# Right-sum transfers into gate and up, border loads and turns in another order, and first sums of an FFN made in the output projection

## The reference

```python
def causal_dwconv(x, w, b):            # width 3 along the tokens, per channel
    ...
def conv_ffn(h, w_gate, w_up, conv_w, conv_b, w_down):
    g = causal_dwconv(h @ w_gate, conv_w, conv_b)
    return (jax.nn.gelu(g) * (h @ w_up)) @ w_down

for i in range(DEPTH):                 # DEPTH = 2, D_FF = 2816
    h = rmsnorm(x, norm_mix[i])
    x = x + mixer(h, ...) @ w_out[i]
    h = rmsnorm(x, norm_ffn[i])
    x = x + conv_ffn(h, w_gate[i], w_up[i], conv_w[i], conv_b[i], w_down[i])
    gate = jax.nn.sigmoid(rmsnorm(x, norm_ple[i]) @ w_ple_gate[i])
    x = x + gate * (p[i] @ w_ple_proj[i])
```

## Time and profile before

| what | value |
|---|---|
| runs | 3158.32, 3159.48, 3169.77 us; median 3159.48 |
| profiled execution, own time | 3161.22 us |
| its span | 3159.2 us |
| PE busy | 3014.0 us, 95% |
| DVE, ACT, POOL busy | 2271.2, 1444.3, 1403.9 us |
| mean granted TensorE clock | 0.979 |

### The profile page before, as it was taken

How to read it: one execution, slowest core, us unless ns; L and a number is a source line. 1 busy time by engine, 2 the same in 40 slices (tenths; PEclk the granted TensorE clock), 3 DMA queues, 4 the chain that set the end, 5 groups by cost and what they waited for, 6 DMA issues and landing times. The chain is left out here.

```text
span 3159.2 us, 44227 instructions
## 1 busy us (share of the span) xinstructions
PE 3014.0 (95%) x14830; PEld 2520.0 (80%) x14830; DVE 2271.2 (72%) x3459; ACT 1444.3 (46%) x3125; POOL 1403.9 (44%) x905
## 2 busy tenths in 40 slices
PE   7999889999999999999899999999998999999989
PEld 6777777989877888878788788899886888878877
DVE  6599957879458887779943332799648888779952
ACT  4384435878343343334432211688633333434431
...
GB/s 179 122 61 164 140 181 122 60 54 78 116 54 80 80 84 82 127 246 193 99 61 37 195 178 170 81 66 80 54 88 54 96 82 80 81 240 197 157 48 53
DMA packets 288086, 349.07 MB, mean 110 GB/s; under 512 B 88316, under 2 KB 181292, under 8 KB 287916
## 3 DMA queue, kind: packets, MB, share of 16 engines
...
## 5 line engine op out<-in xcount | busy, mean ns | idle before, releaser
L2162 DVE TENSOR_SCALAR_CACHE_REDUCE k_x<-k_x,l0in_cand,l0in_want 128x384 bf16<-128x384 f32 (+1 forms) x186 | 175.0, 1004 | 1.2 <-DVE l0in_before L2157 0.2
L78 PE MATMUL l1in_acc<-k_w_lo,k_hi 128*128 128x512 f32 x384 | 151.7, 395 | 5.2 <-POOL k_w_lo L681 2.7
L2648 POOL TENSOR_TENSOR l1ff_w_lo<-l1ff_raw_g,l1ff_w_hi 128x512 fp32r<-128x512 f32 x64 | 93.5, 1466 | 138.6 <-ACT l1ff_w_hi L2511 138.5
L2648 POOL TENSOR_TENSOR l0ff_w_lo<-l0ff_raw_g,l0ff_w_hi 128x512 fp32r<-128x512 f32 x64 | 91.9, 1438 | 140.8 <-ACT l0ff_w_hi L2511 140.7
L2540 ACT ACTIVATE k_x<-k_x 128x512 f32<-128x512 f32 x88 | 55.7, 633 | 212.3 <-DVE k_x L2742 212.3
L79 PE MATMUL l1in_acc<-k_w_hi,k_lo 128*128 128x512 f32 x384 | 150.8, 393 | 0.0
L80 PE MATMUL l1in_acc<-k_w_hi,k_hi 128*128 128x512 f32 x384 | 150.6, 392 | 0.0
L725 DVE TENSOR_TENSOR l1in_sq<-l1in_out 128x512 f32<-128x512 f32 x32 | 40.4, 1264 | 114.7 <-ACT l1in_out L658 114.0
L1619 DVE TENSOR_TENSOR l1dil_pt_lo<-l1dil_ring,l1dil_pt_hi 128x512 fp32r<-128x512 f32 x192 | 101.9, 553 | 4.6 <-ACT l1dil_pt_hi L1555 2.3
L1635 DVE CUSTOM_DVE_ANT_0 l1dil_s<-l1dil_s,l1mix_sliding 128x128 f32<-128x128 f32 (+7 forms) x128 | 97.3, 761 | 9.0 <-PE l1dil_s L1719 4.7
L1555 ACT ACTIVATE l1dil_pt_hi<-l1dil_ring 128x512 fp32r<-128x512 f32 x192 | 92.5, 492 | 22.6 <-PE l1dil_ring L1702 21.4
...
## 6 DMA issues: line engine op xcount, KB each, us to landing
l_right_sums<-in_w_down POOLq DMA_DIRECT2D x24, 1408.0 KB, 14.0
...
k_raw<-in_w_in_odd SPq DMA_DIRECT2D x24, 512.0 KB, 4.9
l0ff_raw_g<-in_w_gate SPq DMA_DIRECT2D x11, 1024.0 KB, 5.2
l0ff_raw_u<-in_w_up SPq DMA_DIRECT2D x11, 1024.0 KB, 5.6
...
l1ff_raw_g<-in_w_gate SPq DMA_DIRECT2D x11, 1024.0 KB, 5.2
```

The costliest lines, as they stand in the source:

```text
L78: pe.matmul(out, a_hi, b_lo, start=start, stop=False)
L2162: tick(dve.tensor_scalar(hits[:, cols], score[:, cols], cand[:, i:i + 1].bitcast(F32), want[:, i:i + 1], ALU.is_ge, ALU.add, accum_out=exc ...
L2648: pool.tensor_tensor(buf.ring_lo[q % R][:], operand(q), buf.ring_hi[q % R][:].bitcast(F32), ALU.subtract).then_inc(w_lo_done[0], 1)
```

## The change

1. The twelve right-sum transfers of each layer leave the input projection. They are issued in gate and up, one each after steps n = 6 and n = 13 of a group, copies in groups 0 to 2, adds in groups 3 to 5.
2. The output stage's POOL program makes the first group's sums for factors 7 and 5 and, for token tiles 4 and 5, the differences that factors 6 and 7 need. The sums are formed in other places: factor 7 in piece (0,0), 5 in piece (1,0), 6 in tmp.
3. The FFN's start has another order: on POOL `root(LAST)` first; on DVE the differences of tile 6 alone, then scale(LAST), and the rest later; on PE turn(LAST) in the middle of step 2 instead of between steps 1 and 2.
4. SP's order at the border of up and down: a11 parts 8 to 10 and a12 part 8 are loaded before the last stores, the parts of a22 and the x tiles one by one between the down loads, and load_down(7) comes right after the last store.
5. The embedding's turns come after parts 7 and 9 of the last down product instead of 6 and 8, and the first waits for all adds but two.

```diff
# projection_stage and project_select_stage, POOL
-                    if s == 1 and t < right_sums.count:
-                        right_sums.copy(pool, t)
-                    if s == 3 and t < right_sums.count:
-                        right_sums.add(pool, t)
...
# SplitFeed
+    def differences(self, engine, t):
+
+        n = t - max(self.first, self.EARLY)
+        front, rear, early = self.raw[self.part(t, 0)], self.raw[self.part(t, 1)], self.raw[self.part(t - self.EARLY, 0)]
+        engine.wait_ge(self.summed, n + 1)
+        engine.wait_ge(self.rested, 2 * max(self.EARLY - self.first, 0) + n + 1)
+        engine.tensor_tensor(front, rear, front, ALU.subtract).then_inc(self.differed, 1)
+        engine.wait_ge(self.differed, 2 * n + 1)
+        engine.tensor_tensor(rear, rear, early, ALU.subtract).then_inc(self.differed, 1)
...
# output_stage, POOL
+            for m in range(2):
+                pool.wait_ge(n_lo_ready, m + 1)
+                pool.tensor_tensor(nxt.piece(m, 0, 0), nxt.piece(m, 0, 0), nxt.piece(m, 1, 0), ALU.subtract).then_inc(n_w_sum, 1)
+                pool.wait_ge(n_w_sum, 2 * m + 1)
+                pool.tensor_tensor(nxt.piece(m, 1, 0), nxt.piece(m, 1, 0), nxt.piece(m, 1, 1), ALU.add).then_inc(n_w_sum, 1)
             for t in range(nxt.ROOTS):
                 nfeed.root(pool, t)
+            for t in range(NT // 2, NT // 2 + 2):
+                nfeed.differences(pool, t)
...
# ffn_stage, SP
+                if q == Q - 1:
+                    sp.wait_ge(filled, Q - 2)
+                    load_part(a11, (0, 0), range(8, 11), a11_in)
+                    load_part(a12, (0, 1), range(8, 9), a12_in[1])
...
-            load_part(a22, (1, 1), range(4, 8), a22_in)
...
             for z in range(DEEP + 3, Z):
                 r, k = divmod(z, KB2)
                 load_down(z)
...
+                if (r, k) == (0, 7):
+                    sp.wait_ge(stored[0], 16 * 2 * NG)
+                    load_part(a12, (0, 1), range(9, 11), a12_in[2])
+                    sp.wait_ge(stored[1], 16 * 2 * NG)
+                    sp.wait_ge(filled, Q)
+                if 8 <= z <= 11 or z in (14, 16, 18, 20):
+                    t = z - 8 if z <= 11 else z // 2 - 3
+                    sp.dma_start(x[:, t, :], buf.kept[t * P:(t + 1) * P, :]).then_inc(x_in[t // 4], 16)
+                if 9 <= z <= 11 or z in (13, 15, 17, 19):
+                    i = z - 5 if z <= 11 else z // 2 + 1
+                    load_part(a22, (1, 1), range(i, i + 1), a22_in)
...
# ffn_stage, POOL
             feed.prepare(pool)
-            add_weights(0, 5, 0)
             feed.root(pool, LAST)
-            add_weights(0, 5, 1)
-            add_weights(0, 7, 0)
+            add_weights(0, 6, 0)
             low(4)
-            add_weights(0, 6, 0)
-            add_weights(0, 7, 1)
+            add_weights(0, 6, 1)
...
+                if n in (6, 13) and grp < 6:
+                    i = 2 * (grp % 3) + (n == 13)
+                    right_sums.copy(pool, i) if grp < 3 else right_sums.add(pool, i)
...
# ffn_stage, PE
-            feed.turn(pe, LAST)
-            step(2)
+            step(2, True)
...
-                if r == len(DOWN) - 1 and k in (6, 8):
-                    if k == 6:
-                        pe.wait_ge(added, ADDED[r])
-                    nfeed.turn(pe, (k - 6) // 2)
+                if r == len(DOWN) - 1 and k in (7, 9):
+                    pe.wait_ge(added, ADDED[r] - 2 if k == 7 else ADDED[r])
+                    nfeed.turn(pe, (k - 7) // 2)
```

More of the change, by code:

```diff
@@ L697, in _ @@
                     low(CH * s + c)
-                    if s in (1, 2) and c < right_sums.count // 2:
-                        right_sums.copy(pool, (s - 1) * (right_sums.count // 2) + c)
-                    if s in (3, 4) and c < right_sums.count // 2:
-                        right_sums.add(pool, (s - 3) * (right_sums.count // 2) + c)
                 if s <= QK:
@@ L1930, in _, with project_select_stage @@
             first.begin(pe, hi, lo)
-def project_select_stage(nc, name, right_sums, hi, lo, strips, proj, vsplit, vstored, room, stats, score, mask, tail, square, decay, first, next_head=None):
+def project_select_stage(nc, name, hi, lo, strips, proj, vsplit, vstored, room, stats, score, mask, tail, square, decay, first, next_head=None):
     S = len(strips)
@@ L2545, in difference, with second_high @@
                     act.wait_ge(t1_lo, 1)
-                    act.wait_ge(t_lo_done, 2)
+                    act.wait_ge(t_lo_done, 3)
                 act.activation(t_hi[f][:], t_raw[f], ACT.Copy).then_inc(t_hi_done, 1)
+            def second_high(n):
+                act.wait_ge(t_sum, 2 + 2 * n)
+                act.activation(t_hi[6][:, :, cols[n]], t_raw[6][:, :, cols[n]], ACT.Copy).then_inc(t_hi_done, 1)
             def split_left(z):
@@ L2589, in _ @@
             feed.square(act, LAST)
+            split(3)
+            second_high(0)
             copy_sum(0, 0)
             feed.round(act, LAST)
-            copy_sum(0, 1)
             act.wait_ge(feed.summed, 1)
             act.activation(hi[:, front, 6 * P:], xt[:, front, 2 * P:4 * P], ACT.Copy).then_inc(t1_hi, 1)
-            for q in range(3, L + 1):
-                split(q)
+            split(4)
+            copy_sum(0, 1)
+            second_high(1)
+            split(5)
             for q in range(1, Q + 3):
@@ L2610, in _ @@
                     base(4 * grp + (n == 12))
[L2611 to L2612 removed]
+                if q in (3, 6):
+                    difference(*{3: (7, 4), 6: (4, 5)}[q])
                 if q + L < Q:
@@ L2824, in down_slot, with sums_of, second_low @@
                     nfeed.rest(dve, (k - 8) // 2)
-            cols = slice(0, 3 * P), slice(3 * P, 4 * P)
-            def difference_sums(n):
+            def sums_of(t):
+                at = slice((t - NT // 2) * P, (t - NT // 2 + 1) * P)
                 b11, b12, b22 = xt[:, front, early], xt[:, front, late], xt[:, rear, late]
-                dve.tensor_tensor(b12[:, :, cols[n]], b22[:, :, cols[n]], b12[:, :, cols[n]], ALU.subtract).then_inc(t_sum, 1)
-                dve.tensor_tensor(b22[:, :, cols[n]], b22[:, :, cols[n]], b11[:, :, cols[n]], ALU.subtract).then_inc(t_sum, 1)
-            difference_sums(0)
-            feed.scale(dve, LAST)
+                n = 2 * (t - LAST + 1)
+                dve.tensor_tensor(b12[:, :, at], b22[:, :, at], b12[:, :, at], ALU.subtract).then_inc(t_sum, 1)
+                dve.wait_ge(t_sum, n + 1)
+                dve.tensor_tensor(b22[:, :, at], b22[:, :, at], b11[:, :, at], ALU.subtract).then_inc(t_sum, 1)
+            def second_low(n):
+                dve.wait_ge(t_hi_done, n + 1)
+                dve.tensor_tensor(t_lo[6][:, :, cols[n]], t_raw[6][:, :, cols[n]], t_hi[6][:, :, cols[n]].bitcast(F32),
+                                  ALU.subtract).then_inc(t_lo_done, 1)
+            sums_of(LAST - 1)
+            feed.scale(dve, LAST)
+            low(3)
+            second_low(0)
+            feed.rest(dve, LAST)
+            dve.wait_ge(t1_hi, 1)
+            dve.tensor_tensor(lo[:, front, 6 * P:], xt[:, front, 2 * P:4 * P], hi[:, front, 6 * P:].bitcast(F32), ALU.subtract).then_inc(t1_lo, 1)
+            dve.wait_ge(feed.rested, 1)
+            dve.wait_ge(feed.summed, 1)
+            sums_of(LAST)
+            low(5)
+            second_low(1)
             dve.wait_ge(kept_stored[0], 16 * 6)
@@ L2838, in _ @@
                 dve.memset(g[i][:, 0:2], 0.0)
-            feed.rest(dve, LAST)
-            dve.wait_ge(feed.rested, 1)
-            dve.wait_ge(feed.summed, 1)
-            difference_sums(1)
-            dve.wait_ge(t1_hi, 1)
-            dve.tensor_tensor(lo[:, front, 6 * P:], xt[:, front, 2 * P:4 * P], hi[:, front, 6 * P:].bitcast(F32), ALU.subtract).then_inc(t1_lo, 1)
-            low(3)
-            low(5)
             dve.wait_ge(cw_t, 1)
@@ L2894, in _, with step @@
         def _(pe):
-            def step(q):
+            def step(q, turn=False):
                 grp, f, m = op(q)
@@ L2920, in step @@
                 for k in range(4):
+                    if turn and k == 2:
+                        feed.turn(pe, LAST)
                     mm = mm3(pe, out(grp, f, m), buf.ring_hi[q % R][:, k, :], buf.ring_lo[q % R][:, k, :], b_hi[:, k, :], b_lo[:, k, :],
@@ L3011, in trunk @@
                                   second_at=MERGED_AT + 8 * KB)
-                    projection_stage(nc, L + "in", right_sums[layer], x, heads, ident, proj, vsplit, vstored, stats, dil)
+                    projection_stage(nc, L + "in", x, heads, ident, proj, vsplit, vstored, stats, dil)
                 recycle(nc)
```

80 lines of the change are left out of this document (28 added, 52 removed).

## The result

The changed kernel takes 3135.6 us (median of 5 runs, 3133.9 to 3138.9) against 3158.3 for the kernel before (5 runs): ratio 0.9931, interval 0.9918 to 0.9944. It is faster by 22.7 us. I had forecast 3071, a gain of 88.9 on the 3159.5 of the first three runs, in a range of 3058 to 3106. Where the other 65 us went is the subject of what follows.

A forecast was written before the change was run, and what follows sets the result against it. PE, busy 95% of the span, was taken as the bound, so only its waits counted. Gains 29.5 + 3.8 + 2 x (11.6 + 7.8 + 8.4) = 88.9 off 3159.5 gave 3071 us, range 3058 to 3106.

The forecast's parts named there:

- Right sums in gate and up: In gate and up, 24 right-sum transfers issued one at a time, about 19 us apart, would cost 0.
- The sign that I had named for it: Would show the forecast wrong: a new PE wait for w_lo behind DMA at the heads of groups 1 to 6.
- My upper bound of 14.1: In gate and up, a 5.2 us weight load stretched by 13.3/4.9 beside a transfer would take 14.1, 8.9 more.
- The slack: Gate and up: the second group's load is there about 7.4 us early, so 1.5 of 8.9 would show.
- The right sums cost in gate and up what they cost in the projection: Rival for gate and up: 24 transfers at 1.5 to 2.5 cost 36 to 60, 3107 to 3131 us; chance 0.08.
- Layer 0's projection: Without transfers, PE's three waits at strip heads (22.7) and 7.5 after them go, less about 0.6: gain 29.5 us.
- slow part: What a PE wait costs after its end: 2.5 us for over 4, 1 to 1.6 for 2.7, none under 2.
- the search's cover: In layer 0's projection, DVE's top-k search would still end before ACT, by 1.8 us.
- Layer 1's projection: One PE wait of 2.7 for k_w_lo, with 1.1 lost after it, goes: gain 3.8 us.
- The FFN's start: Step 1 to 12 falls from 48.4 to 34.7 us, less 1.8 at the output stage's end: gain 11.6 per layer.
- The border: From up to down, PE's 5.52 us wait goes as load_down(7) is issued earlier: gain 7.8 per layer.
- The end of down: PE's 8.53 us wait before the next stage's first turn shrinks to 2.2: gain 8.4 per layer.

The follow-up runs named there:

- the quiet places: Changed kernel with copies moved behind steps n = 0 and 1 of groups 1 to 3, adds behind n = 0 of groups 4 to 9: 3078.3 us, ratio 0.9745.

## Why the prediction was wrong

**The step that failed** is "Right sums in gate and up", priced at 0: "One transfer at a time is nearer to layer 1's projection than to layer 0's, so I take 0." It measured 26.8 and 25.9 us in groups 1 to 10 of the two layers, and with the transfers at the quiet places the kernel is 57 us faster. The sign that I had named for it came, a new wait of PE for w_lo, at the heads of groups 2 to 6. Without this cost the time comes near what I had forecast, 3078.3 against 3071. Part of that is luck, since misses cancel: by the profiles of that run and of before, layer 0's projection gave 34.1 where I had 29.5, and the two FFN stages 23.9 and 21.3 where I had 27.8 each.

Three things in that step were wrong. The first could have been read beforehand from the order of POOL's program; for the other two I had bounds from rows and took the mild end.

1. *The place.* I had the transfers "about 19 us apart, beside loads that are issued once in 38", as if they met by chance. They don't: the one behind n = 6 stands in POOL's written order right ahead of the low half that releases the next group's gate load. It goes out 6.6 us ahead of the load in group 0 and 2.0 to 2.5 ahead in groups 1 to 5. The runs that keep one place each show it.
2. *The stretch.* From issue to ACT a gate load takes 5.1 to 6.7 us alone in the kernels before and after. Those issued in groups 1 to 5 took 9.3 to 9.9 beside copies and 11.7 to 13.6 beside adds (1086.90 to 1098.90 above). My upper bound of 14.1 was about right for the adds, and even the copies, one at a time, were far from free. The Trainium skill ("DMA: Bandwidth & Descriptors", Queues, rings and completion order) has each DMA engine take turns between queues packet by packet. By that rule alone, with packets that take equally long, I would estimate at most twice 5.4: the copies keep to it, the adds don't.
3. *The slack.* I took 7.4 us from rows 10 and thought of it as there in every group. It is a stock in a loop: load, sums and halves, release of the next load. How far ahead of PE's next group gate's load reaches ACT (its lead), group by group (layer 0, groups 1 to 10, us, from the timelines):

```
before       9.6  9.4  8.8 10.0 10.8 11.4 11.5 11.6 11.5 11.6
sums away    5.8  6.2  7.2  8.2  9.2  9.8 10.9 11.3 11.2 11.4
after        4.8  2.1  2.0  2.0  2.0  2.0  5.3  5.1  6.8  8.1
```

2.0 is what the two halves need; there PE waits. The second row is the changed kernel with the right sums in the projections. From step 1 on, the shorter start of the FFN moves PE ahead by 9.7 us but gate's load by only 6.2 (39.1 behind step 1 before, 32.9 after), so without any transfer the changed kernel begins with 3.8 to spare (5.8 less 2.0), not 7.4, and the loop wins back about 1 us a group. Every stretch of 4 to 8 us falls on that. The two parts of the change took from the same stock, and I had costed each with the other away. But the transfers drain a larger start too: the kernel before with the transfers moved began with 8.4 of lead and was down to 2.0 by group 4. PE waited less for POOL's halves there, 5.6 instead of 14.7, but DVE's late halves held it back too, so what the larger start was worth alone can't be read from that run. That the loop wins back so little is read from these rows; no run changed its length by itself. I had no term either for what each wait costs after its end, 11.2 of the 26.8 in layer 0.

**The rivals.** The one that held was "The right sums cost in gate and up what they cost in the projection", at 0.08: 24 at 1.5 to 2.5, 3107 to 3131. They cost 53 / 24 = 2.2 each, or 5.3 for each of the ten that meet a load head on, with 3135.6 for the whole, 4.6 over the top of that rival, as the FFN's start gave less too. That I gave it a chance of 0.08 was the second error: my upper bound (8.9 of stretch against 7.4 of slack) already said that it must cost if one transfer stretches like two, and the trace of before had no row against that.

**Point by point.**
- *Layer 0's projection*, 29.5: 32.5 between the two profiles. The stretch up to the attention was 515.6 to 519.7 in four kernels with the transfers in it and 484.4 to 486.8 in eight without, 32 in the mean. Right: the waits, their slow part and the search's cover.
- *Layer 1's projection*, 3.8: 4.6 between the two profiles. But with the transfers in it the stretch was 276.0, 273.0, 276.7 and 271.5 in four kernels that don't differ there, and 269.8 to 271.4 without. The gain is 0 to 7 and its mean, 3.4, about what I had.
- *The FFN's start*, 11.6 a layer: step 1 to 12 is 38.6, not 34.7, and the boundary costs 2.4, not 1.8; 7.4 in all (8.2 in layer 1). DVE is what ends the stage, as I had it: beside POOL's differences (the first row is one) four of its operations take 1.57, 1.76, 1.18 and 1.74 instead of 0.69, 3.5 in all. But this makes a wait of PE of 3.06, which brings a slow part that I had not charged: the 12 matmuls of step 1 (887.68 to 892.13) take 4.45 instead of 2.72.

```profile
877.97 2.20 POOL L773 TENSOR_TENSOR l0ff_xt<-l0ff_xt 128x512 f32<-128x512 f32 x1 [1.42 <-DVE l0ff_lo L804]
...
879.15 1.57 DVE L808 TENSOR_TENSOR l0ff_xt<-l0ff_xt 128x512 f32<-128x512 f32 x1
880.64 1.76 DVE L804 TENSOR_TENSOR l0ff_lo<-l0ff_xt,l0ff_hi 128x512 fp32r<-128x512 f32 x1
...
883.52 1.18 DVE L808 TENSOR_TENSOR l0ff_xt<-l0ff_xt 128x512 f32<-128x512 f32 x1
884.63 1.74 DVE L804 TENSOR_TENSOR l0ff_lo<-l0ff_xt,l0ff_hi 128x512 fp32r<-128x512 f32 x1
886.29 0.68 DVE L999 TENSOR_TENSOR l0ff_lo<-l0ff_xt,l0ff_hi 128x512 fp32r<-128x512 f32 x1
887.68 0.50 PE L78 MATMUL l0ff_bank_u<-l0ff_lo,l0ff_w_hi 128*128 128x512 f32 x1 [3.06 <-POOLq L2668]
892.13 0.40 PE L78 MATMUL l0ff_bank_g<-l0ff_lo,l0ff_w_hi 128*128 128x512 f32 x1
926.30 0.47 PE L78 MATMUL l0ff_bank_g<-l0ff_t_lo,l0ff_w_hi 128*128 128x512 f32 x1 [0.96 <-issue]
```

 The run without the four operations gives 3.3 a layer back. The Trainium skill ("GPSIMD Engine Reference", 1. Specifications) has GpSimd contend with VectorE operations of this kind, without a price. The trace agrees, and the 3.5 of the rows is nearer to the 4 that I had estimated for contention in full than to my 1.8.
- *The border*, 7.8 a layer: 4.9 alone (6.6 and 3.3; 13.7 us over two layers in runs of the same chip, noise of some us in it). The wait went as I said, smaller ones came.
- *The end of down*, 8.4: 7.7, with the wait at 2.1. Right.
- Border and end together, 16.2: 13.1 and 11.0 in the changed kernel, 16.5 and 13.3 with the quiet places, so 2 to 3 us a layer of the transfers' cost reached past gate and up. The first group of down waits 2.6 and 1.1 for its right operand there, and nothing with the quiet places. The traces fit the stock: of the 24 FFN stages profiled here, that wait is 1.1 to 2.6 in eight, all with a lead of 7.5 to 9.4 at group 10, and under 0.7 in every one with a lead of 9.7 or more; one (lead 9.2, wait 0.5) is in between. No run tests it by itself.
